# The residual kept turned through both layers: output products with weights loaded, no turns at five borders, all xbc blocks in three passes

## What is computed

```
for i in range(2):
    x = x + 0.5 * swiglu(rms_norm(x, ffn1_norm[i]), w_gate, w_up, w_down)   # 1024 -> 2816 -> 1024
    h = rms_norm(x, mix_norm[i])
    z, xbc, dt_raw, q, k, v = split(h @ w_in[i])
    y_ssd = ssd_mixer(silu(conv(xbc)), dt_raw, z, ...)
    y_att = dilated_attention(rms_norm(q), rms_norm(k), v)
    x = x + concatenate([y_ssd, y_att]) @ w_out[i]
    x = x + 0.5 * swiglu(rms_norm(x, ffn2_norm[i]), ...)
x = second_block(x, ...)
```

## Time and profile before

| | us |
|---|---|
| median of 3 runs | 2091.73 (2088.2 to 2092.58) |
| the profiled execution | 2090.46 |
| its span in the profile | 2088.7 |
| busy PE | 2048.2 |
| busy PE weight loads | 1833.4 |
| busy DVE | 1647.5 |
| busy ACT | 1211.7 |
| busy POOL | 456.0 |

### The profile page before, as it was taken

How to read it: one execution, slowest core, us unless ns; L and a number is a source line. 1 busy time by engine, 2 the same in 40 slices (tenths; PEclk the granted TensorE clock), 3 DMA queues, 4 the chain that set the end, 5 groups by cost and what they waited for, 6 DMA issues and landing times. The chain is left out here.

```text
span 2088.7 us, 35595 instructions
## 1 busy us (share of the span) xinstructions
PE 2048.2 (98%) x13737; PEld 1833.4 (88%) x13737; DVE 1647.5 (79%) x2070; ACT 1211.7 (58%) x1527; POOL 456.0 (22%) x237
## 2 busy tenths in 40 slices
PE   9999999999999999999999999999999999999997
PEld 8998999789999998999789998999877877777775
DVE  5776767567766875868557766998699999999998
ACT  5434465653435434565554335444378888888886
POOL 4992000007931990000007920000000000000000
PEclk9999999999999999999999999999999999999999
DMA  8875554247865774554257754445669999999994
GB/s 264 281 257 164 162 162 146 97 148 243 265 229 176 261 257 153 173 154 157 81 170 236 268 171 132 142 126 174 256 247 370 367 370 373 369 373 370 370 367 182
DMA packets 238937, 483.67 MB, mean 232 GB/s; under 512 B 10612, under 2 KB 178976, under 8 KB 222464
## 3 DMA queue, kind: packets, MB, share of 16 engines
q1 hardware_dynamic: 226880, 443.58, 60.7%
q0 software_dynamic: 11360, 37.21, 5.3%
q10 hardware_dynamic: 608, 1.65, 0.2%
HBM read 481.31 MB, written 1.09 MB: 231 GB/s over the span
## 5 line engine op out<-in xcount | busy, mean ns | idle before, releaser
L798 PE MATMUL misc<-xhl,ring_low 128*128 128x256 f32 x1536 | 425.4, 277 | 0.0
L797 PE MATMUL misc<-xhl,high_b 128*128 128x256 f32 x1344 | 372.6, 277 | 0.0
L799 PE MATMUL misc<-xhl,high_b 128*128 128x256 f32 x1344 | 371.6, 277 | 0.0
L798 PEld LDWEIGHTS misc<-xhl,ring_low 128*128 128x128 f32 x1536 | 288.9, 188 | 3.4
L3087 DVE TENSOR_TENSOR ring_low<-ring,high_b 128x2048 fp32r<-128x2048 f32 x128 | 287.2, 2285 | 0.6 <-issue 0.6
L1812 ACT ACTIVATE arena<-arena 128x256 f32<-128x256 f32 x88 | 36.8, 418 | 418.2 <-DVE arena L2423 418.2
L2384 DVE TENSOR_TENSOR ring_low<-ring,high_b 128x2048 fp32r<-128x2048 f32 x88 | 252.8, 2908 | 8.1 <-ACT high_b L1781 7.4
L797 PEld LDWEIGHTS misc<-xhl,high_b 128*128 128x128 f32 x1344 | 252.3, 188 | 3.4
L2132 ACT ACTIVATE high_b<-ring 128x2048 fp32r<-128x2048 f32 x124 | 235.8, 1914 | 29.7 <-DMA ring<-in_w_dram 28.8
L799 PEld LDWEIGHTS misc<-xhl,high_b 128*128 128x128 f32 x1344 | 252.4, 188 | 0.0
L1692 POOL TENSOR_SCALAR arena<-arena,cact 128x1024 f32<-128x1024 f32 x56 | 214.5, 3831 | 4.5 <-DMA arena<-in_w_ada_dram 1.4
(11 more groups left out here) (471 smaller groups left out, 5167.9 us busy)
## 6 DMA issues: line engine op xcount, KB each, us to landing
ring<-in_w_dram SPq DMA_DIRECT2D x128, 1024.0 KB, 7.7
ring<-in_w_in_dram SPq DMA_DIRECT2D x72, 1024.0 KB, 5.5
ring_d<-in_w_dram SPq DMA_DIRECT2D x128, 512.0 KB, 5.1
ring<-in_ffn_w_gate_dram SPq DMA_DIRECT2D x44, 1024.0 KB, 5.5
ring<-in_ffn_w_up_dram SPq DMA_DIRECT2D x44, 1024.0 KB, 8.1
ring_d<-in_ffn_w_down_dram SPq DMA_DIRECT2D x88, 512.0 KB, 7.3
arena<-in_w_ada_dram POOLq DMA_DIRECT2D x48, 512.0 KB, 5.1
ring<-in_w_out_dram SPq DMA_DIRECT2D x20, 1024.0 KB, 4.9
```

What stands on the lines that cost most here:

```text
L797: pe.matmul(dst, wh, ml, start=start, stop=False, **kw)
L798: pe.matmul(dst, wl, mh, start=False, stop=False, **kw)
L799: return pe.matmul(dst, wh, mh, start=False, stop=stop, **kw)
```

## The change

The residual is kept turned (`xT`, 1024 features on the partitions in 8 tiles, in the memory of `xnT`) from the start to the end of FFN 3. The output products of FFN 0 to 2 and of `w_out` load the weights and let the hidden values move, so that they add to a turned accumulator `accT` in the same banks: 24 products of 128x256 in place of 12 of 128x512. FFN 3 keeps the old form.

At the five borders the 16 transposes go. `add_turned` adds four pairs of tiles, each as soon as PE has finished it; ACT and DVE form `xh` and `xl` from SBUF tile by tile, and `first_block` takes them in that order. The sum of squares comes from a pass of ACT over `xT`, three additions on DVE (`sums`), one product with a matrix of ones inside the next `gate_up` or the second xbc block (`row_of_sums`), a root on ACT and a reciprocal of the whole row on DVE. In FFN 0 to 2 DVE scales gate and up together. All xbc blocks have three passes; the weight blocks behind each border are split before it. At the start DVE also copies the turned `x` to `xT`. Before the last product of FFN 3 PE turns the residual back (`rows_again`). POOL multiplies `xT` by the mixer's gain into the memory of `x` (`rows_for_steps`), for the small dt product.

```diff
+        xT = xnT[:, :, :]
...
-        X_SPLIT = 6
+        X_SPLIT = 8
...
+            def rows_again():
+
+                m0 = FILL["rows"]
+                for q in range(4):
+                    t, half = divmod(q, 2)
+                    b = claim_bank(m0 + q)
+                    for c in range(4):
+                        mm = pe.transpose(b[:, c * P:(c + 1) * P], xT[:, half * 4 + c, t * P:(t + 1) * P], ident)
+                    mm.then_inc(filled, 1)
...
+            def row_of_sums(u):
+
+                pe.wait_ge(sums_ready, u)
+                mm = pe.matmul(acc[:, 0, 0:SEQ], ones[:, :], squared[:, 0:SEQ], start=True, stop=True,
+                               skip_group_check=True)
+                for t in range(NT if u in COLUMNS_TOO else 0):
+                    mm = pe.matmul(acc[:, 0, SEQ + t:SEQ + t + 1], squared[:, t * P:(t + 1) * P], ones[:, 0:1],
+                                   start=True, stop=True, skip_group_check=True)
+                mm.then_inc(row_done, 1)
...
+            def first_block(u, parts, b):
+
+                xh, xl = rows_at[u]
+                before = tiles_before(u)
+                for k in range(KD):
+                    pe.wait_ge(xh_ready, before + k + 1)
+                    for g, (wh, wl) in enumerate(parts):
+                        to = b[:, g * SEQ:(g + 1) * SEQ]
+                        pe.matmul(to, wh[:, k, :], xh[:, k, :], start=(k == 0 and g == 0), stop=False,
+                                  skip_group_check=True)
+                        pe.matmul(to, wl[:, k, :], xh[:, k, :], start=False, stop=False, skip_group_check=True)
+                for g, (wh, wl) in enumerate(parts):
+                    for k in range(KD):
+                        pe.wait_ge(xl_ready, before + k + 1)
+                        mm = pe.matmul(b[:, g * SEQ:(g + 1) * SEQ], wh[:, k, :], xl[:, k, :], start=False,
+                                       stop=(k == KD - 1), skip_group_check=True)
+                return mm
...
+            def down_turned(m0, n0, d0, f, i, c, start, stop, between=()):
+                g0 = NF * f
+                hidh, hidl = hid_at[f]
+                pe.wait_ge(hid_low, i * 4 + (g0 + c + 1))
+                dn = d0 + c
+                wait_split_d(pe, low_in_d, d0, i, c)
+                q = (m0 + c) % 2
+                for k in range(KD):
+                    ks = slice(k * P, (k + 1) * P)
+                    mm = three(accT[:, k, :], high_r[:, dn % SLOTS, ks], ring_d_low[:, dn % SLOTS, ks], hidh[:, q, :],
+                               hidl[:, q, :], start and k % 2 == 0, stop, skip_group_check=True)
+                    if c % 2 == 0 and k < 2:
+                        mm.then_inc(freed[(n0 + c + k) % SLOTS], 1)
+                    if stop and k % 2 and k < KD - 1:
+                        mm.then_inc(acc_half, 1)
+                    if stop and k == KD // 2 - 1:
+                        for p in between:
+                            modulation(p)
+                mm.then_inc(freed_d[dn % SLOTS], 1)
...
                 pe.wait_ge(row_ready, u + 1)
-                down(m0, n0, d0, f, 0, 0, True, False)
+                summed = down_turned if f < 2 * DEPTH - 1 else down
+                summed(m0, n0, d0, f, 0, 0, True, False)
 
                 with pe.Fori(0, (NF - 2) // 4) as i:
                     for j in range(4):
                         gate_up(m0, n0, u, i, j + 2)
-                        down(m0, n0, d0, f, i, j + 1, False, False)
+                        summed(m0, n0, d0, f, i, j + 1, False, False)
+                if not f:
+                    params()
+                if f == 2 * DEPTH - 1:
+                    rows_again()
                 for p in pieces[:1]:
                     modulation(p)
-                down(m0, n0, d0, f, 0, NF - 1, False, True, pieces[1:])
+                summed(m0, n0, d0, f, 0, NF - 1, False, True, pieces[1:])
...
+                first_block(3 * l + 1, [(high_part(n0)[:, :, c * P:(c + 1) * P], low_part(n0)[:, :, c * P:(c + 1) * P])
+                                        for c in range(2)], b).then_inc(freed[n0 % SLOTS], 1)
+                for j in range(1, 8):
                     wait_split(pe, low_in, n0 + j)
                     b = claim_bank(FILL["xbc", l] + j)
-                    wh, wl = high_w_part(j - 8), low_part(n0 + j)
...
+                            if (j, c, k) == (1, 0, KD - 1):
+                                pe.wait_ge(acc_free, a)
+                                row_of_sums(3 * l + 1)
...
+                def out_row(k, tiles):
+                    n = n0 + k // 2
                     w = rows_part(n)
...
+                    for dt in tiles:
+                        ds_ = slice(dt * P, (dt + 1) * P)
+                        if k < PLAIN:
+                            mm = pe.matmul(accT[:, dt, :], w[:, k % 2, ds_], yT[:, k, :], start=(k == 0 and dt % 2 == 0),
+                                           stop=False, skip_group_check=True)
+                        else:
...
                 for k, c in rows_left:
-                    out_rows(k, [c]).then_inc(freed[(n0 + k // 2) % SLOTS], 1)
+                    out_rows(k, c).then_inc(freed[(n0 + k // 2) % SLOTS], 1)
                 modulation(4 * l + 1)
-                out_rows(14, [0])
-                out_rows(15, [0]).then_inc(acc_half, 1)
-                out_rows(14, [1])
-                out_rows(15, [1]).then_inc(freed[(n0 + 7) % SLOTS], 1)
+                row_in(14)
+                row_in(15)
+                for dt in range(KD):
+                    out_row(14, [dt])
+                    mm = out_row(15, [dt])
+                    if dt % 2 and dt < KD - 1:
...
+            def rows_for_steps(l):
+
+                if not l:
+                    for i in range(4):
+                        wait_drained(pool, FILL["params"] + i)
+                for k in range(KD):
+                    pool.wait_ge(x_ready, PAIRS * 3 * l + k // 2 + 1)
+                    ins = pool.tensor_scalar(xn[:, k, :], xT[:, k, :], cola[:, l, C_MIX + k:C_MIX + k + 1], None, ALU.mult)
+                ins.then_inc(xn_ready, 1)
 
             for j in range(SLOTS):
...
+                if u:
+                    for k in range(KD):
+                        act.wait_ge(x_ready, PAIRS * (u - 1) + k // 2 + 1)
+                        act.mul(xh[:, k, :], xT[:, k, :], gain(k)).then_inc(xh_ready, 1)
...
                 ffn(2 * l + 1, 3 * l + 2)
+            for q in range(4):
+                t, half = divmod(q, 2)
+                m = FILL["rows"] + q
+                wait_filled(act, m)
+                act.activation(x[:, t, half * 512:(half + 1) * 512], bank_of(m), ACT.Copy).then_inc(drained[m % 4], 1)
...
                                                        op1=ALU.subtract)
-                    ins.then_inc(drained[(m0 + q) % 4], 1)
+                    ins.then_inc(xl_ready, 1)
+                    dve.tensor_copy(xT[:, 2 * q:2 * q + 2, :], b.rearrange("p (a b) -> p a b", a=2))\
...
+            def sums(u):
+
+                dve.wait_ge(squares_in, u)
+                for n_ in (4, 2):
+                    link(dve.tensor_tensor(squared[:, 0:n_ * SEQ], squared[:, 0:n_ * SEQ],
+                                           squared[:, n_ * SEQ:2 * n_ * SEQ], ALU.add))
+                dve.tensor_tensor(squared[:, 0:SEQ], squared[:, 0:SEQ], squared[:, SEQ:2 * SEQ], ALU.add)\
+                    .then_inc(sums_ready, 1)
+
+            def root_of_row(u):
+
+                dve.wait_ge(std_ready, u + 1)
+                w = SEQ + (NT if u in COLUMNS_TOO else 0)
+                link(dve.reciprocal(row_cols[:, 0:w], row_cols[:, 0:w]))
+                dve.nop().then_inc(rstd_ready, 1)
+                dve.nop().then_inc(row_ready, 1)
...
+                up = hid[:, q, :] if f < 2 * DEPTH - 1 else bank_of(m)[:, SEQ:2 * SEQ]
+                dve.tensor_tensor(hid[:, q, :], up, gate_s[:, q, :], ALU.mult).then_inc(drained[m % 4], 1)
...
-                    dve.tensor_tensor(gate_s[:, q, :], bank_of(m0 + j)[:, 0:SEQ], row_rstd[:, :], ALU.mult)\
-                        .then_inc(gate_scaled, 1)
+                    if f < 2 * DEPTH - 1:
+                        dve.tensor_tensor(gate_and_up[:, q, :, :], bank_of(m0 + j).rearrange("p (a b) -> p a b", a=2),
+                                          row_rstd.unsqueeze(1).to_broadcast([P, 2, SEQ]), ALU.mult)\
+                            .then_inc(gate_scaled, 1)
...
+                    chunk(0, c, c < NF - 2 or f < 2 * DEPTH - 1)
...
+            def add_turned(u, factor, wait_last, between=()):
+
+                for q in range(PAIRS):
+                    if q == PAIRS // 2:
+                        for p in between:
+                            modulation(p)
+                    if q < PAIRS - 1:
+                        dve.wait_ge(acc_half, (PAIRS - 1) * (u - 1) + q + 1)
+                    else:
+                        wait_last()
+                    ks = slice(2 * q, 2 * q + 2)
```

(9 more changed lines are left out.)

213 lines of the change are left out of this document (116 added, 97 removed).

## The result

The changed kernel takes 2100.6 us (2097.92 to 2105.27, six runs), the kernel before 2092.15 in the same comparison: ratio 1.004, 95% interval 1.002 to 1.0059. It is slower by 8.5 us where 8.1 less were forecast, and outside the stated range of 2076 to 2092. The profiled execution took 2100.26 us with a span of 2098.5, 9.8 more than before.

The account below looks back on a forecast made before the run. PE was taken as the bound inside chunks, with waits at the borders. Terms for products, start, borders, end and chunks summed to -8.1 us from 2090.46; with 1.3 for the median, 2083.6 us, range 2076 to 2092.

Parts of the forecast that it names:

- What bounds the kernel: Inside chunks PE is the bound, without gaps, gate and up products taking 0.1138 us each; waits stand at the borders.
- The products themselves: Output products of 66 chunks and two `w_out` stages, 24 of 128x256 at 0.1138 us each: -1 us.
- above 0.12: Sign of a wrong forecast: new products pacing above 0.12 us; 0.006 more on some 1,900 is 11 us.
- Inside the chunks: DVE's chain 0.27 us longer, 5 late places in FFN 0 to 2 at 0.5 us each: +2.5 us.
- rival A: POOL's multiplications hold DVE's second operand fully, making `xl` late at borders 4 and 1: 2090 to 2094, chance 0.13.
- rival B: DVE sets the pace of FFN 0 to 2 chunks where POOL runs: 21 us cost, about 2102, chance 0.08.
- Start: Four PSUM copies of `x` before the low part that PE awaits in FFN 0: +1.8 us, bounds 1 and 2.8.
- Borders 1 to 5: Time from the old stage's last product to the first common one: -6.1, -0.7, -1.9, -4.1 and -0.4 us.
- the chain that was worked out for border 3: Additions, `xl` steps, sums, row, root, reciprocal and `low_rows` end at T+13.2, against 15.11 us for the border before.
- The 0.8 us for the root and its signals: Estimate at border 3 for the root on ACT with signals, between the row at T+7.0 and the reciprocal.
- The 1.6 us for the clock: Part of border 1's gain: full clock expected where granted clock was 0.66 between 200 and 205 us.
- end: Sixteen transposes added at the end of FFN 3, all on PE: +1.8 us, bounds 1.7 and 2.3.

Follow-up runs that it names:

- experiment 4: The changed kernel run again unchanged for a second profile, compared with the kernel before: 2100.67 us, ratio 1.0032.
- Experiment 8: The kernel before with only its 512-column output products each made as two of 256 columns: 2100.35 us, ratio 1.0037 to the kernel before.
- experiment 9: The changed kernel with the low part ahead of the long reciprocal and up scaled in the addition, no products cut: 2098.45 us, ratio 1.0035 to the kernel before.
- Experiment 5: The changed kernel with up read from PSUM again and scaled only in the addition to the residual: 2102.78 us, ratio 1.0034 to the kernel before.
- experiment 3: The changed kernel with the last product of each output product of FFN 0 to 2 cut in two: 2098.24 us, ratio 1.0031 to the kernel before.
- experiment 7: The changed kernel with low part ahead of the reciprocal, every second output product cut, and up scaled in the addition: 2086.66 us, ratio 0.9963 to the kernel before.

## Why the prediction was wrong

- **What bounds the kernel.** "There is no gap; inside the chunks PE is the bound" was right. That 0.1138 is the pace of this form of product was not. It is a mean over two paces, some seven products at 0.118 and the rest at 0.1134, and the earlier trace rows gave it because in that kernel PE came back to the quick one behind the 512-column products, which the change removes from FFN 0 to 2. This is where the prediction fails.
- **"The products themselves", -1 us.** This is the step that failed. In the state of 113.4 ns the term is even better than forecast (8.16 for 8.21, 66 x 0.05 = 3.3 us). But 72 products of a chunk, those of gate and up included, can run 4.4 ns slower: 0.32 us a chunk. I had priced "above 0.12" as the danger for 1,900 new products; it was 0.118, and it can fall on any of the 4,752 in FFN 0 to 2. In the profile it fell on the last third of FFN 0, on all of FFN 1 and on FFN 3. In place of -1 the chunks of the four networks, without their waits, give some +11 us, in this profile and in that of experiment 4. Experiment 8 puts the loss at 9 us for the form of the output product alone; experiment 9 has 15 us of pace in FFN 0 to 2 where nothing brings it back. The Trainium skill (TensorE: Matmul & The Clock Gate, section Back-to-back issue gap) gives a warm product N/2.4 + 2.5 ns, as the gap of an isolated one, and says that in a stream of weight loads and products both set the distance; the prediction applied the 2.5 ns to every product and left that out. The traces show 6.7 ns above 256 cycles at 2.4 GHz in one state and 11.1 in the other, so by that figure neither state could have been told.
- **"Inside the chunks", +2.5 us.** The place was right, the size was 7.2. I charged 0.27 us for the scaling and took the margins from before. The multiplication also collides with POOL now, 0.28 us more on average and up to 2.0, and the subtraction takes 836 ns in place of 557. Experiment 5 shows that the two together are the cause. The Trainium skill (SBUF — State Buffer, section Who interferes with whom) has the rule: a DVE instruction with two SBUF inputs contends with a POOL instruction that reads SBUF; the trace agrees, 424 ns beside POOL with one operand in PSUM, 870 with none, and 425 with none where no POOL record lies beside. I had weighed that rule for border 4 (rival A), where 0.48 us a step was no loss, and named it in rival B, at 0.08. B's mechanism holds at a price of 5 us more than forecast, not 21.
- **Start, +1.8.** Measured +2.9, of which 1.7 are a stretch of 3.4 us at half the clock (1.2 GHz) that begins at 19.0; in the second profile, where no such stretch falls there, the first output product starts at 26.94, +1.1.
- **Borders 1 to 5.** -6.4, -0.5, -1.4, -4.3, -0.4 against -6.1, -0.7, -1.9, -4.1, -0.4: right, with the chain that was worked out for border 3, and with a granted clock of 1.00 from 200 to 205 us. The 0.8 us for the root and its signals had no row behind it; PE's record of the row ends at 652.83 and the reciprocal starts at 653.38, 0.55 us. The 1.6 us for the clock hold as well: the two profiles with transposes at border 1, those of the kernel before and of experiment 8, have a stretch at half clock there (200.8, 204.0), the other 12 have none. The **end** was right, too: the transposes stand from 1262.82 to 1264.56, 1.7 us.
- **Not foreseen**: 0.6 and 0.8 us in the mixers, where the products of `w_out` now start 118.3 and 118.6 ns apart, more than half of the 231.8 that one of 512 columns took. The second block is 0.9 us shorter, and before it had a stretch of 3.4 us at half the clock (1269.19), so up to 0.8 us are longer there; its pace sum is 2.7 us in both, and the cause is not shown.

What is open: what in PE holds one pace or the other. Weight load and product alternate in the same way in both states (the load starts some 3 ns behind the start of the product before it), and the same disturbance ends in either: behind the waits of 1.85 us in front of the first output product, FFN 1 goes on at 0.118 (463.76) and FFN 2 at 0.113 (659.12), in one profile. The runs show places where it changes, not why. That the form of the output product costs 9 us is shown by experiment 8; by what it does so, the width of its products, its doubled weight loads or their place in the row, is open.

## What to carry to other kernels

A start-to-start distance is a property of the whole row of instructions, not of the instruction: before replacing a form of product, ask what the old one did for its neighbours, and look for places in the trace where the same product runs at another distance (here the mixers, at 0.118, were in view). When a change saves at the borders and loses in the loop, compare loop bodies at first: 0.32 us in each of 66 chunks outweighs five good borders. Where DVE shares time with POOL, leave one operand in PSUM. Before a safeguard is put in everywhere, count how often it finds something to repair: 6 of 66 cuts did in experiment 3, two in experiment 7.
